# A hybrid decoder step on one core: the block branch of the prompt inside the compression, a tile-wise first projection, and whole cache pages per transfer

## The reference

```python
def rmsnorm(x, g):
    return x * rsqrt(mean(x * x, -1) + EPS) * g
def chunk_gmlp(x, w_in, ...):
    uv = gelu(rmsnorm(x) @ w_in); u, v = uv[..., :D_A], uv[..., D_A:]
    ...
def compress(rows, pos_k, pos_v, w_k, w_v, k_norm):      # 32 rows every 16 rows -> 31 blocks
    kc = einsum('bnlgd,lde->bnge', blk[:, :, :, 0] + pos_k, w_k)
    vc = einsum('bnlgd,lde->bnge', blk[:, :, :, 1] + pos_v, w_v)
    return rmsnorm(kc, k_norm), vc
def cmp_branch(q_n, q_pos, kc, vc):                      # the "block branch"
    s = einsum('btgrd,bngd->btgrn', q_n, kc) * ATTN_SCALE
    p = masked_softmax(s, blk_end <= q_pos)              # 31 blocks a head, 16 heads, 4 key groups
    return einsum('btgrn,bngd->btgrd', p, vc)
o = gates[0] * o_cmp + gates[1] * o_slc + gates[2] * o_win
```

## Time and profile before

| | |
|---|---|
| time of three runs | 1720.08, 1718.71, 1720.0 us, median 1720.0 |
| the profiled execution | 1722.8 us, of which the span is 1721.0 |
| mean granted PE clock | 0.979 |
| PE busy | 1638.5 us, 95% of the span |
| DVE, ACT, POOL busy | 863.2, 554.1, 82.1 us |
| DMA | 156.73 MB, mean 91 GB/s |

### The profile page before, as it was taken

The page is one execution under the profiler, slowest core; times in us unless marked ns, Lnnn a source line. Parts: engine busy times, 40 slices in busy tenths (PEclk is TensorE's granted clock), DMA queues, the critical chain, the costliest instruction groups (busy, mean ns, idle before and its releaser), DMA issues.

```text
span 1721.0 us, 31983 instructions
## 1 busy us (share of the span) xinstructions
PE 1638.5 (95%) x13058; PEld 1505.4 (87%) x13058; DVE 863.2 (50%) x1400; ACT 554.1 (32%) x942; POOL 82.1 (5%) x137
## 2 busy tenths in 40 slices
PE   5998999999999999999998679999889999999998
PEld 5998999999999999999887446666579999999998
DVE  3326654455444344263276558896446444433433
ACT  4334321233212112153335426675343222212111
POOL 0000000000000000000000004452000000000000
PEclk8999999999999999999999969999999999999999
DMA  4347212233232332222234340004532232222311
GB/s 131 97 144 259 68 63 74 91 96 98 73 98 73 98 94 78 80 67 99 74 108 120 102 147 1 2 2 146 149 74 76 96 98 75 96 90 82 98 55 70
DMA packets 139312, 156.73 MB, mean 91 GB/s; under 512 B 11738, under 2 KB 127762, under 8 KB 138802
## 3 DMA queue, kind: packets, MB, share of 16 engines
q1 hardware_dynamic: 139138, 155.42, 28.5%
q10 hardware_dynamic: 80, 0.02, 0.0%
HBM read 149.58 MB, written 14.16 MB: 95 GB/s over the span
## 4 chain that ended last, share of the span: by engine, by line
PE 90%; DVE 4%; SPq 2%; ACT 2%; issue 1%; DMA 1%; DVEq 0%; ACTq 0%
PE PS L569 60%; PE PS L597 12%; PE PS L956 2%; PE PS L943 2%; PE PS L929 2%; PE PS L604 1%; PE PS L738 1%; PE PS L864 1%; SPq L511 1%; PE PS L910 1%; SPq L513 1%; PE PS L1043 1%; PE PS L1009 1%; PE PS L610 1%; DMA cache<-in_state_kv_win 1%
## 5 line engine op out<-in xcount | busy, mean ns | idle before, releaser
L569 PE MATMUL PS<-act0h,wh 128*128 128x272 f32 x1664 | 345.4, 289 | 2.7 <-DVE sg L1684 2.7
L569 PE MATMUL PS<-act0l,wh 128*128 128x272 f32 x1664 | 344.1, 288 | 0.0
L569 PE MATMUL PS<-act0h,wl 128*128 128x272 f32 x1664 | 343.8, 288 | 0.0
L1135 ACT ACTIVATE wh<-raw 128x2048 fp32r<-128x2048 f32 x106 | 202.8, 1914 | 407.2 <-PE PS L569 407.1
L1497 DVE TENSOR_TENSOR wl<-raw,wh 128x2048 fp32r<-128x2048 f32 x106 | 243.1, 2294 | 174.8 <-ACT wh L1135 174.3
L569 PEld LDWEIGHTS PS<-act0h,wh 128*128 128x128 f32 x1664 | 259.9, 188 | 3.3 <-issue 2.8
L569 PEld LDWEIGHTS PS<-act0l,wh 128*128 128x128 f32 x1664 | 259.8, 188 | 0.0
L569 PEld LDWEIGHTS PS<-act0h,wl 128*128 128x128 f32 x1664 | 259.7, 188 | 0.0
L1530 DVE TENSOR_TENSOR hT<-PS,hT 128x544 f32 (+1 forms) x72 | 52.1, 724 | 214.7 <-PE PS L569 214.0
L597 PE MATMUL PS<-wh,act0h 128*128 128x256 f32 x448 | 130.4, 291 | 10.6 <-DVE sel_v L1607 10.6
L597 PE MATMUL PS<-wh,act0l 128*128 128x256 f32 x448 | 126.6, 283 | 0.0
(11 more groups left out here) (296 smaller groups left out, 2502.4 us busy)
## 6 DMA issues: line engine op xcount, KB each, us to landing
raw<-in_ffn_w_gate SPq DMA_DIRECT2D x44, 512.0 KB
raw<-in_ffn_w_up SPq DMA_DIRECT2D x44, 512.0 KB
raw<-in_a_w_in SPq DMA_DIRECT2D x32, 512.0 KB
raw<-in_ffn_w_down SPq DMA_DIRECT2D x32, 512.0 KB
raw<-in_a_w_out SPq DMA_DIRECT2D x16, 512.0 KB
crows<-in_cache_kv_cmp SPq DMA_DIRECT2D x64, 128.0 KB, 2.1
cache<-in_cache_kv_slc SPq DMA_DIRECT2D x32, 256.0 KB, 5.1
cache<-in_state_kv_win SPq DMA_DIRECT2D x8, 1024.0 KB, 8.2
```

The source lines that it names most:

```text
L569: mm = pe.matmul(PS[:, 4 * ps + 2 * mt + h, 0:HALF], W[:, rs, k, mt * P:mt * P + P], Xp[:, k * T + h * HALF:k * T + h * HALF + HALF], star ...
L1135: act.activation(wh[:, rs, :, :], raw[:, rs, :, :], ACT.Copy).then_inc(w_hi, 1)
```

## The change

Three edits, each in its own place.

1. **First block tile-wise.** The halves of the activations are made for the first 256 tokens as soon as two token tiles are stored (`first_high`, `first_low`, 8 pieces of 256 tokens), with the first weight block's halves after the second piece; the rest (288 tokens) follows when all tiles are stored. SP issues the first weight block ahead of x tiles 2 to 4. PE makes item 0 one token tile after another. The transposes use four PSUM banks rather than eight.
2. **Pages whole.** A sample's page is fetched once, keys and values together, 32 DMAs of 256 KB (each row 2 KB) into five buffers; the first two samples are issued ahead of the compression weights.
3. **Block branch inside the compression.** POOL builds block-diagonal keys `kbd` (two key groups of a pair in 64 columns), so a query tile takes 8 products of 64 columns over all 128 rows. Tile 3 is done in round 2, tile 2 in round 3, tile 1 in round 4 and tile 0 in round 5. DVE masks, takes maxima and inverse sums; POOL subtracts and scales; ACT takes the exponentials, one tile a round. Then `vcz` is filled in step i = 3 of the attention's list on ACT, and `Qbd` is cleared by POOL and filled by ACT in steps 8 to 15.

```diff
-    crows = [... [P, 4, PAGES, 256]) for j, a in enumerate((A_RAW, A_WL))]
+    crows = [... [P, PAGES, 512]) for j, a in enumerate((A_RAW, A_RAW + 8192, A_WL, A_WL + 8192, A_WH + 8192))]
-    ecmp = at("ecmp", A_P0 + 8192, [P, 4, NH, 32])
+    ecmp = [at(f"ecmp{j}", a, [P, NH, 32]) for j, a in enumerate((...))]
+    kbd = kvtok[:, 3, 256:384].rearrange("p (a n) -> p a n", a=2)
...
 # SP
+            if t == 1:
+                segment_few(at_v, a_w_in[0], DA, 0, 0, 1)
...
+        def cmp_cache(b):
+            j = b % len(crows)
+            if b >= len(crows):
+                sp.wait_ge(c_tr, groups_of(3)[b - len(crows)] + 1)
+            pages(crows[j], cache_kv_cmp, b, c_load[j])
+        sp.wait_ge(w_ready, at_wo[0] + 2)
+        sp.wait_ge(f_mm, 18)
+        for b in range(2):
+            cmp_cache(b)
         sp.wait_ge(halves, 2 * (at_q[1] + 4))
...
+        for b in range(2, NB):
+            cmp_cache(b)
 # PE
+            if fresh == 0:
+                pe.wait_ge(free[ps], 2 * use + 2)
+                for t in range(QT):
+                    for k in range(KT):
+                        if t % 2 == 0:
+                            pe.wait_ge((e_split, xn_ready)[t // 2], k + 1)
+                        mm = products(t, k)
+                    if t == 2:
+                        pe.wait_ge(f_ready, 1)
+                        partials()
...
+            if n >= 4:
+                pe.wait_ge((x_evd, x_eva)[n % 2], (n - 4) // 2 + 1)
...
+        def block_scores(y):
+            qt = CUNITS - 1 - y
+            if y % 2 == 0:
+                pe.wait_ge(n_ms, y // 2)
+            else:
+                pe.wait_ge(vc_done, y - 2)
+            if y == BLOCK_FROM:
+                pe.wait_ge(b_kd, 5)
+            for k in range(KT):
+                mm = pe.matmul(PS[:, 7, 64 * k:64 * k + 64], qTn[:, k, qt * P:qt * P + P], kbd[:, k // R, :], start=True, stop=True)
+            mm.then_inc(b_s, 1)
...
+                if y >= BLOCK_FROM and l == (6 if y == BLOCK_FROM else 2):
+                    block_scores(y)
...
-        cmp_finish(CUNITS - 1)
-        block_scores()
         for i in range(HALVES + 5):
             if i < HALVES:
                 scores(i)
+            if i == 1:
+                cmp_finish(CUNITS - 1)
             if i == 2:
+                pe.wait_ge(vc_done, 5)
                 block_turn()
                 pe.wait_ge(z_fill, R)
 # ACT
+            if t == 1:
+                act.wait_ge(x_evd, 2)
+                act.wait_ge(x_eva, 2)
+                for k in range(2):
+                    first_high(k, 0)
+                split(0, 0, 0)
+                for k in range(2, KT):
+                    first_high(k, 0)
...
+            if y > BLOCK_FROM:
+                block_exps(y - 1 - BLOCK_FROM)
...
+            if i == 3:
+                fill()
+                act.wait_ge(z_q, 1)
+            if 8 <= i < 16:
+                sample_queries(i - 8)
 # DVE
+            if y > BLOCK_FROM and i == (3 if y == BLOCK_FROM + 1 else 2):
+                block_mask(y - 1)
...
+            if y >= BLOCK_FROM:
+                block_maxima(y)
+            if y > BLOCK_FROM:
+                block_sums(y - 1 - BLOCK_FROM)
...
         maxima(0)
+        block_sums(QT - 1)
 # POOL
+        for j in range(QT):
+            for n, ready, op, done in ((0, b_mx, ALU.subtract, b_sh), (1, b_f, ALU.mult, b_p)):
+                if j == QT - 1 and n == 0:
+                    pool.memset(vcz[:, :, :, :], 0.0).then_inc(z_set, 1)
+                    pool.wait_ge(c_mm, CUNITS)
+                    pool.memset(Qbd[:, :, :, :, :], 0.0).then_inc(z_q, 1)
+                e = ecmp[j][:, :, 0:NCMP]
+                pool.wait_ge(ready, j + 1)
+                pool.tensor_tensor(e, e, cstat[:, n, j, :].unsqueeze(2).to_broadcast([P, NH, NCMP]), op).then_inc(done, 1)
```

More of the change, by code:

```diff
@@ L1239, in _, with first_high @@
         flat = xs[:, :, :].rearrange("p k t -> p (k t)")
+        def first_high(k, g):
+            h = hT[:, k, 2 * P * g:(2 * P, T)[g]]
+            act.activation(first(act0[0], k, g), h, ACT.Copy, scale=gains[:, k:k + 1]).then_inc((e_high, xh_ready)[g], 1)
         for t in range(TT):
@@ L1389, in _, with fill, sample_queries @@
                 cmp_finish(y - 1)
+        block_exps(QT - 1)
         cmp_finish(CUNITS - 1)
-        act.wait_ge(z_set, 2)
-        for r in range(R):
-            act.activation(vcz[32 * r:32 * r + NCMP, :, r, :], vc[:, 0, :].rearrange("n (g d) -> n g d", g=NG),
-                           ACT.Copy).then_inc(z_fill, 1)
+        def fill():
+            act.wait_ge(z_set, QT + 1)
+            for r in range(R):
+                act.activation(vcz[32 * r:32 * r + NCMP, :, r, :], vc[:, 0, :].rearrange("n (g d) -> n g d", g=NG),
+                               ACT.Copy).then_inc(z_fill, 1)
+        def sample_queries(j):
+            kind, p, g2 = j // 4, j // 2 % 2, j % 2
+            q, g = (qTn, qTr)[kind], 2 * p + g2
+            dst = Qbd[64 * g2:64 * g2 + 64, kind, p, :, 16 * g:16 * g + 16].rearrange("q b (r t) -> q b r t", r=R)
+            src = q[64 * g2:64 * g2 + 64, R * p:R * p + R, TP:T].rearrange("q r (b t) -> q b r t", b=NB)
+            act.activation(dst, src, ACT.Copy).then_inc(q_bd, 1)
         def exps(v):
@@ L1428, in _ @@
                 act.wait_ge(s_out, OUTS)
-                for qt in range(QT):
-                    act.wait_ge(b_pt, qt + 1)
-                    act.activation(PTc[:, qt, :], PS[:, 4 + qt, :], ACT.Copy).then_inc(b_pe, 1)
+                for j in range(QT):
+                    act.wait_ge(b_pt, j + 1)
+                    act.activation(PTc[:, QT - 1 - j, :], PS[:, 4 + j, :], ACT.Copy).then_inc(b_pe, 1)
             if 3 <= i < HALVES + 3:
@@ L1611, in _, with first_low @@
         dve.memset(stats[:, C_MS:80], 1.0).then_inc(st_set, 1)
+        dve.memset(PS[:, 3, 0:CW], 0.0).then_inc(st_set, 1)
+        dve.wait_ge(s_cst, 16)
+        selector(sel_v, 0)
+        def first_low(k, g):
+            dve.wait_ge((e_high, xh_ready)[g], k + 1)
+            dve.scalar_tensor_tensor(out=first(act0[1], k, g), in0=hT[:, k, 2 * P * g:(2 * P, T)[g]], scalar=gains[:, k:k + 1],
+                                     in1=first(act0[0], k, g).bitcast(F32), op0=ALU.mult,
+                                     op1=ALU.subtract).then_inc((e_split, xn_ready)[g], 1)
         for n in range(0, 2 * TT, 2):
-            if n == 4:
+            if n == 2:
                 dve.wait_ge(g_set, 1)
-                dve.tensor_copy(gains[:, :], PS[:, 7, 0:40]).then_inc(g_set, 1)
+                dve.tensor_copy(gains[:, :], PS[:, 3, 0:40]).then_inc(g_set, 1)
             dve.wait_ge(x_tr, n + 1)
@@ L1618, in _ @@
             dve.tensor_copy(dst, src).then_inc(x_evd, 1)
-        dve.wait_ge(g_set, 2)
+            if n == 2:
+                dve.wait_ge(g_set, 2)
+                dve.wait_ge(x_evd, 2)
+                dve.wait_ge(x_eva, 2)
+                for k in range(2):
+                    first_low(k, 0)
+                split(0, 0)
+            if n in (4, 6):
+                for k in range(2 + 3 * (n - 4) // 2, 5 + 3 * (n - 4) // 2):
+                    first_low(k, 0)
         dve.wait_ge(x_evd, TT)
@@ L1622, in _ @@
         for k in range(KT):
-            low(act0, 0, k, k)
-        split(0, 0)
-        selector(sel_v, 0)
+            first_low(k, 1)
         split(1, 1)
```

194 lines of the change are left out of this document (84 added, 110 removed).

## The result

The changed kernel took 1694.79 us (median of four runs, 1693.94 to 1695.63), the kernel before 1719.36 beside it (1717.98 to 1720.08, four runs). The ratio is 0.9861, 95% interval 0.9846 to 0.9876: 24 us less, between 21 and 26. The forecast was 1688 and 31.7 us less. The profiled execution took 1695.63 (span 1693.8), against 1722.8 (span 1721.0): 27.2 less.

A forecast was written before the change was run, and what follows sets the result against it. PE, busy at 9 tenths, was taken as the bound, so only its idle, half-clock or removable work could give time. 7.2 + 4.4 + 21.9 - 1.8 = 31.7 us gained: 1691.1 profiled, 1688 median, range 1680 to 1700.

The forecast's parts named there:

- The forecast's chain: Start: from ACT's store of tile 1 through halves and last turns to PE's first product at 17.4, gaining 7.2 us.
- Sum: 9.4 - 4.0 - 1.0 = 4.4 gained: Compression rounds: page waits removed, less added block scores, less a round 4 wait for mean squares, in us.
- about 43: Sign to look for in the compression: rounds 3 to 5 together take about 43 us.
- the text's own signs of being wrong: PE waiting for DVE in rounds 3 and 4, another releaser than the fill, a stalled start item, or a longer attention half.
- The transfers' term: Compression: 32 whole-page transfers need 36 us instead of 72, arrive in time, and PE's 9.4 us of waits go.
- a round 1.0: Compression: eight 64-column block score products cost PE 1.0 us a round, at most 1.8; 4.0 in four rounds.
- 1.0 (0 to 4): Round 4: block scores wait 1.0 us for DVE's mean squares, bounds 0 to 4.
- eight times 1.2 us: Rounds: POOL reading SBUF locks out DVE's two-input instructions, 9.6 us in all; if half counts, 1693.
- rival 2: Compression: DVE and ACT set the rounds, nothing gained there (-4.4), plus the port's price (-5): 1697; chance 0.23 with the port rule.
- 24.8 + 1.8 = 26.6: Last compression product to first value product: 24.8 us at warm rows instead of 46.7, plus 1.8 for half clock.
- Rivals 1, 3 and 4: Clock helps more, 1683, 0.16; whole pages do not help, 1697, 0.06; block tiles' ring over POOL slower, 1721 to 1723, 0.03.
- the cover for ACT's fill of `Qbd`: Attention steps 8 to 15: ACT's 8 x 0.3 us lie beside PE's work; failing that they cost 2.4.

The follow-up runs named there:

- `pages_only`: The kernel before with only whole pages (keys and values fetched together) added: 1707.84 us, ratio 0.9932.
- `block_only`: The changed kernel with the old first block and the old half pages put back: 1702.72 us, ratio 0.9910.
- `changed_again`: The changed kernel itself, unaltered, run again on another chip: 1694.39 us, ratio 0.9859 to the kernel before.
- `double_columns`: The changed kernel with 128 instead of 64 moving columns in each block score product: 1692.64 us, ratio 0.9850 to the kernel before.
- `rope_first`: The changed kernel with DVE's block maxima and sums moved behind the rotation in every round: 1690.61 us, ratio 0.9836 to the kernel before.
- `best`: The changed kernel with rotation first, mean squares early, `vcz` fill early, and the second norm's rest moved to round 5: 1683.51 us, ratio 0.9800 to the kernel before.
- `fill_early`: The changed kernel with ACT's fill of `vcz` moved two steps ahead, before the exponentials of half 1: 1690.65 us, ratio 0.9835 to the kernel before.
- `best_again`: The same kernel as `best`, run again beside the changed kernel on one chip: 1683.75 us, ratio 0.9793 to the kernel before.
- `ms_early`: The changed kernel with the second norm's mean squares at the head of DVE's list in round 4: 1690.63 us, ratio 0.9840 to the kernel before.

## Why the prediction was right, and where it failed

**First block: right in size, not in its parts.** Forecast 7.2, and PE is 7.16 ahead at the gate products (905.13 to 897.97) and 7.10 at the first compression turn; the part alone measured 6.7 (3.6 to 8.4 by its interval, 0.9979 and 0.9951 of 1719.4). The agreement to 0.1 us is luck of this pair. The first product came 8.2 earlier, but some 2 us of that belong to the one execution of before: it waited 6.6 us for its first x tile, `pages_only` and `block_only` with the same start 4.7, and their first products stand at 22.42 and 22.61. The forecast's chain, which began at 10.92, was read from that late execution; in the changed kernel ACT had stored tile 1 by 8.78 + 0.60 = 9.38. With the new start the first product stands between 15.60 and 17.89 in nine profiles, so about 7 us ahead of the three with the old start. PE's wait for DVE's tile `bd` near 145 us, 2.0 in this profile and 0.5 in that of before, is no cost of the new start either: it is 1.8 in `pages_only` with the old start and 0.5 in `changed_again` with the new. At the turns behind the gate products (L788 and L801) the three profiles with the old start stand at 909.54 to 911.02 and the nine with the new at 901.84 to 905.24, by their means 7.1 apart.

**Rounds: the failed step.** "Sum: 9.4 - 4.0 - 1.0 = 4.4 gained" was 2.55 lost, and rounds 3 to 5 took 48.3 us (945.64 to 993.92) instead of "about 43". One of the text's own signs of being wrong came: PE waited for DVE among the products of round 4. The transfers' term held: 12.4 by itself (75.02 to 62.65, 9.4 of it the waits). The block work was priced at 5.0 and costs 14.9. Its terms, with what they measured:
- the scores, "a round 1.0": 1.73, so 6.9 in four rounds instead of 4.0. What failed is the scaling of a row of 512 columns down to 64; `double_columns` shows a floor by instruction. The upper bound (1.8) held.
- the wait in round 4, "1.0 (0 to 4)": 3.53. DVE's own list accounts for 1.85, which is what `rope_first` leaves; 1.66 of the rotation products in round 4 (2.56 - 0.90) is POOL's share, which it removes. The text had weighed this as a rule of the Trainium skill (SBUF — State Buffer, Who interferes with whom) and given it to a rival. The rows agree with the rule: 0.90, 1.75, 2.56 us. Its "eight times 1.2 us" was too much, since only some of POOL's instructions meet a DVE instruction that reads SBUF twice: 0.85 + 1.66 + 1.66 = 4.2 us, and of these only the 1.66 of round 4 reached PE.
- the granted clock, for which the rounds had no term: 2.6 us in round 4 (the scores' extra 1.74 and the products behind them until about 972), and 1.7 at the head of round 5 (11.07, against 9.38 in `best`), 4.3 in all. This is the largest of the three misses, and in round 4 it varies between executions.

6.9 + 3.5 + 4.3 = 14.7 of the 14.9. So the waits for `crows` went as forecast, but rival 2 (DVE sets the rounds, with the port's price) was half there beside it, and its "nothing gained in the rounds" is nearer to what came than the 4.4 gained. The total says the same: 1694.8 lies outside the 1684 to 1694 to which the forecast gave 0.52, 6.8 us above its 1688 and 2.2 below rival 2's 1697. It is inside the range because the range took in the rivals. The parts that do not add up when each is run alone are another matter: the forecast had priced pages and block work together.

**Tail: right.** 24.8 + 1.8 = 26.6 was forecast, 25.48 measured, a gain of 21.2 for 20.1. PE stood before the scores of step 3 for the fill, forecast about 5 us, measured 3.70, and `fill_early` shows that the fill was the cause. The fill ended at 1011.59, 17.67 behind the last product, for 17.8 forecast. The clock stood at 0.50 in part of it, as chosen.

**Table loads.** The trace of after has six switches between root and exponential in the compression, one of them here:

```profile
967.22 0.41 ACT L1402 ACTIVATE kvtok<-kvtok 128x248 f32<-128x248 f32 x1 [4.97 <-DVE kvtok L1942]
967.65 1.28 ACT L1413 ACT_TABLE_LOAD   x1
```

The load begins 0.02 us behind the end of the instruction ahead (967.22 + 0.41), as in the earlier trace rows; the next instruction begins at 968.94, 0.01 behind the end of the load. The Trainium skill's drain of 1.38 us (ScalarE: Activation LUTs, What ACT_TABLE_LOAD costs) shows in none of the six loads. The row decides.

**Rivals 1, 3 and 4.** The clock did not stay high in the tail (0.50 from 1012 to 1014). Whole pages came in time: PE waits for none. POOL's instruction took 1.02 us (1.2 in the forecast), far from the 10 at which the ring would decide.

The sum at the first value product: 7.1 - 2.55 + 21.2 = 25.8 (1045.17 to 1019.40). By the last value product of the attention it is 25.05 (1182.87 to 1157.82): 0.5 is lost at the second value product and 0.2 near the middle of the attention, and nothing in steps 8 to 15, so the cover for ACT's fill of `Qbd` held. The samples gain the other 2.1 of the span's 27.2, 1.6 of it in 20 us where the clock was 0.91 before (1190 to 1210) and 1.00 after (1164 to 1184). It was 0.94 from 1160 to 1190 in `changed_again`, so this is likely a difference of executions and no gain of the change; no run isolates its cause. The medians differ by 24.6, since the profiled execution of before lies 3.4 above its median and that of after 0.8.

## What to carry to other kernels

Two edits that work on the same stretch need not add up: here one took waits away, the other filled them, and each alone was worth what its own theory gave it. Price them on the stretch as it is with the other one in. Scale a row down by columns only after looking for a floor by instruction, and before giving work to POOL look which DVE instructions with two SBUF inputs will stand beside it: here the order of DVE's list decided it, at no cost. When an engine waits near a clock step, put the one short instruction that releases it at the head of the list: in four of five profiles the wait cost again in half clock behind it. And read a row that starts a forecast in more than one execution: the start of before was 2 us late in the only one that was profiled.

## What the runs showed of the hardware that I had not expected

- Products with 64 and with 128 moving columns take the same time on PE, 1.89 and 1.90 us for 16 instructions at full clock.
- Four DVE instructions of 128x128 from two SBUF inputs take 0.90 us alone, 1.75 beside one POOL instruction of 1.02 us and 2.56 beside two. POOL's two took 2.05, and 2.00 beside DVE's joins.
- A PE wait of 1.85 us in round 4 was enough for the clock to fall behind it (`rope_first`), while the wait of 2.27 us for ACT's store at the end of round 4, which is the same in all of them, was followed by full clock in `pages_only`, `double_columns`, `rope_first`, `fill_early`, `best` and `best_again`, and by some us of half clock in the changed kernel, `changed_again`, `block_only` and `ms_early`; that is worth 1.7 us each time (11.07 against 9.38). The longer wait of 3.53 us was followed by full clock in `double_columns`. What decides it no run here isolates.
